# Turning queries and keys of the neighbourhood attention with VectorE blocks and on-chip transfers instead of TensorE transposes

## What is computed

```
q, k, v = split(h @ w_qkv, 3)                 # 256 x 2048 each, 16 heads of 128
q = rms_norm(q per head, q_gain); k = rms_norm(k per head, k_gain)
s[q, i, j] = q . k(row i, column j of the window) * 128**-0.5 + bias   # 4 rows x 16 columns
out = softmax(s) @ v;   x = x + out @ w_o
```

## Time and profile before

| what | value |
|---|---|
| median of three timed runs | 2403.22 us |
| the profiled execution | 2403.74 us |
| its span (first to last instruction) | 2402.0 us |
| TensorE busy | 2390.1 us, 100% by the page's rounding |
| VectorE busy | 1528.0 us, 64% |
| ScalarE busy | 1225.9 us, 51% |
| GpSimd busy | 106.2 us |
| hardware queue of SyncE's transfers | 58.6% of the 16 DMA engines' span |
| granted TensorE clock | full speed in all slices but a rounding |

### The profile page before, as it was taken

One profiled execution on the slowest core, in us unless ns is written; L12 is line 12 of the kernel. 1 busy time (PEld: TensorE's weight loads), 2 busy tenths in 40 slices (PEclk: granted clock), 3 DMA queues, 4 the chain that ended last, 5 costly groups with the idle time before them and its releaser, 6 DMA issues.

```text
span 2402.0 us, 30494 instructions
## 1 busy us (share of the span) xinstructions
PE 2390.1 (100%) x12340; PEld 2045.0 (85%) x12340; DVE 1528.0 (64%) x1788; ACT 1225.9 (51%) x1597; POOL 106.2 (4%) x117
## 2 busy tenths in 40 slices
PE   8999999999999999999999999999999999999999
PEld 7998988788888888888877888888888888888887
DVE  6767866577567657667666655655655654564654
ACT  6555455555445445545565655555443443443442
POOL 0221410000000000000000100000000000000000
PEclk9999999999999999999999999999999999999999
DMA  9566786555655656655655665555556566666664
GB/s 307 152 170 175 167 206 206 167 186 191 202 183 181 206 174 196 201 178 189 216 183 167 187 190 171 158 175 185 184 193 193 183 196 193 191 190 195 185 202 149
DMA packets 327068, 451.69 MB, mean 188 GB/s; under 512 B 14464, under 2 KB 209280, under 8 KB 326288
## 3 DMA queue, kind: packets, MB, share of 16 engines
q1 hardware_dynamic: 324640, 440.52, 58.6%
q0 software_dynamic: 2144, 9.22, 2.4%
q10 hardware_dynamic: 144, 0.01, 0.0%
HBM read 446.54 MB, written 2.10 MB: 187 GB/s over the span
## 4 chain that ended last, share of the span: by engine, by line
PE 99%; DVE 0%; DMA 0%; ACT 0%; SPq 0%; issue 0%; POOL 0%; DVEq 0%
PE main L585 94%; PE aux L585 3%; PE aux L598 1%; PE aux L699 0%; PE aux L717 0%; DMA RAW<-in_w_in 0%; DVE LO L1189 0%; DVE AR L1192 0%; DVE XT L1192 0%; PE aux L683 0%; DVE AR L1189 0%; PE aux L659 0%; ACT HI L834 0%; PE aux L608 0%; SPq L529 0%
## 5 line engine op out<-in xcount | busy, mean ns | idle before, releaser
L1189 DVE TENSOR_TENSOR LO<-RAW,HI 128x1024 fp32r<-128x1024 f32 (+2 forms) x833 | 1010.7, 1236 | 594.7 <-ACT HI L834 594.2
L834 ACT ACTIVATE HI<-RAW 128x1024 fp32r<-128x1024 f32 (+2 forms) x833 | 851.2, 1045 | 642.8 <-PE main L585 591.9
L585 PE MATMUL main<-XT,HI 128*128 128x512 f32 x2944 | 739.5, 393 | 0.0
L585 PE MATMUL main<-HI,YT 128*128 128x512 f32 x2240 | 693.2, 389 | 0.0
L585 PEld LDWEIGHTS main<-XT,HI 128*128 128x128 f32 x2944 | 530.0, 189 | 95.6 <-issue 0.2
L585 PEld LDWEIGHTS main<-HI,YT 128*128 128x128 f32 x2240 | 420.5, 188 | 86.9
L585 PE MATMUL main<-HI,XT 128*128 128x512 f32 (+1 forms) x1472 | 456.2, 385 | 7.6 <-DVE LO L1189 7.6
L585 PE MATMUL main<-LO,YT 128*128 128x512 f32 x1120 | 435.8, 389 | 0.0
L585 PEld LDWEIGHTS main<-XT,LO 128*128 128x128 f32 x2944 | 401.6, 190 | 28.8
L585 PE MATMUL main<-XT,LO 128*128 128x256 f32 x2944 | 410.4, 282 | 0.0
L585 PEld LDWEIGHTS main<-HI,XT 128*128 128x128 f32 x1472 | 274.8, 188 | 58.4 <-DVE XT L1192 7.0
(11 more groups left out here) (91 smaller groups left out, 730.1 us busy)
## 6 DMA issues: line engine op xcount, KB each, us to landing
RAW<-in_mlp_w SPq DMA_DIRECT2D x256, 512.0 KB, 4.2
RAW<-in_w_up SPq DMA_DIRECT2D x176, 512.0 KB, 4.9
RAW<-in_na_w_qkv SPq DMA_DIRECT2D x96, 512.0 KB, 4.4
RAW<-in_w_in SPq DMA_DIRECT2D x95, 512.0 KB, 4.6
RAW<-in_w_down SPq DMA_DIRECT2D x88, 512.0 KB, 4.6
RAW<-in_w_out SPq DMA_DIRECT2D x32, 512.0 KB, 4.5
RAW<-in_w_ple_gate SPq DMA_DIRECT2D x32, 512.0 KB, 4.5
RAW<-in_na_w_o SPq DMA_DIRECT2D x32, 512.0 KB, 4.2
```

The source lines that it names most:

```text
L585: return L.e.matmul(out, l, r, start=start, stop=stop, skip_group_check=True)
L834: return L.e.activation(out, x, f, **kw)
L1189: return L.e.tensor_tensor(out, x, y, op)
```

## The change

Queries and keys no longer go through TensorE to be turned.

- VectorE multiplies into one QN and then does one transpose instruction on it that turns each 32 by 32 block in place within the block's 32 partitions, into QB (128 partitions, 4 pieces of a head, 256). For the queries the order within a block is reversed.
- SyncE carries the blocks to their partitions: 16 transfers from SBUF to SBUF for each query or key block, each of 32 partitions with two runs of 512 bytes, into QL (queries; the place of SQN) or KG (keys). They stand in SyncE's queue ahead of the fetch of the ninth slot after the block's last (`turned_heads`), behind a wait for VectorE's transpose. For the four groups these are fetches 464, 488, 512, 536 (queries) and 472, 496, 520, 544 (keys).
- The two gains and 128**-0.5 are multiplied into one vector, once (`head_gains`), and put on the queries alone: ScalarE copies QL to QG with that scale at slot j0 + 13 (`n_gain`, 128x1024).
- `n_score` reads the keys of a head in five runs of 32, 128 elements apart, and waits for ScalarE's `n_gain` and for the transfers of the keys. Scores and norms move one slot later, the first two heads' probabilities from j0 + 24 to j0 + 26 and their products from 26 to 27, the other two's from 26 and 28 to 27 and 29.
- TensorE's and VectorE's `n_turn` are gone, all 16 of each. ScalarE's squares of a key block wait for `n_gain` of the group, VectorE's transpose waits until the transfers before it have landed.

```diff
         for grp in range(4):
             j0 = 448 + 24 * grp
-        for i in range(2):
-            for t in range(2):
-                put(mid, j0 + 10 + 8 * i + t + (grp + i == 0), "n_turn", grp, i, t)
+        put(mid, j0 + 13, "n_gain", grp)
...
+            def turned_heads(grp, i):
+                L.wait_ge(S("v_nt"), 2 * grp + i + 1)
+                if grp and i:
+                    L.wait_ge(S("p_ns"), 4 * grp)
+                for p in range(4):
+                    for d in range(4):
+                        dst = (QL, KG)[i][32 * d:32 * d + 32].rearrange("p (t c) n -> p t c n", t=2)[:, :, p if i else 3 - p, :]
+                        src = QB[32 * p:32 * p + 32, d, :].rearrange("p (t n) -> p t n", t=2)
+                        L.e.dma_start(dst, src).then_inc(S("d_nt"), 16)
+
+            moved = {b.last + 9: b.what[1:] for b in blocks if b.what[0] == "qk"}
             for j in range(len(slot)):
                 if j < 4:
                     turned_input(j)
+                if j in moved:
+                    turned_heads(*moved[j])
                 fetch(j)
...
-                q, k = QG[grp % 2][:, hh, :], KG[grp % 2][:, hh, :]
+                q, k = QG[:, hh, :], KG[:, :, 32 * hh:32 * hh + 32]
                 out = take("n_score", h)
-                L.wait_ge(S("v_nx"), 4 * grp + 4)
-                mm(out[:, 0:160], q[:, 0:128], k[:, 96:256], True, True)
-                mm(out[:, 160:320], q[:, 128:256], k[:, 0:160], True, True).then_inc(S("p_ns"), 1)
+                L.wait_ge(S("a_ng"), grp + 1)
+                L.wait_ge(S("d_nt"), 512 * grp + 512)
+                mm(out[:, 0:160], q[:, 128:256], k[:, 3:8, :], True, True)
+                mm(out[:, 160:320], q[:, 0:128], k[:, 0:5, :], True, True).then_inc(S("p_ns"), 1)
...
+            def n_gain(grp):
+                L.wait_ge(S("v_gk"), 1)
+                L.wait_ge(S("d_nt"), 512 * grp + 256)
+                if grp:
+                    L.wait_ge(S("p_ns"), 4 * grp)
+                act(QG.rearrange("p h (g n) -> p g h n", n=32), QL.rearrange("p g (h n) -> p g h n", n=32), ACT.Copy, scale=gqk).then_inc(S("a_ng"), 1)
...
-                    if i > 1:
-                        L.wait_ge(S("p_nt"), 2 * (i - 2) + 2)
-                    tt(QN[i % 2], p8, bc(nr, 2, 128), ALU.mult).then_inc(S("v_nn"), 1)
+                    if i:
+                        L.wait_ge(S("v_nt"), i)
+                    tt(QN, p8, bc(nr, 2, 128), ALU.mult).then_inc(S("v_nn"), 1)
+                    L.wait_ge(S("v_nn"), i + 1)
+                    if i:
+                        L.wait_ge(S("d_nt"), 256 * i)
+                    turned = QB.rearrange("p k (m n) -> p k m n", n=32)
+                    L.e.transpose(turned if i % 2 else turned[:, :, :, ::-1], QN.rearrange("p m (k n) -> p k m n", n=32)).then_inc(S("v_nt"), 1)
```

More of the change, by code:

```diff
@@ L216, in stages @@
         j0 = 448 + 24 * grp
-        for i in range(2):
-            for t in range(2):
-                put(mid, j0 + 10 + 8 * i + t + (grp + i == 0), "n_turn", grp, i, t)
+        put(mid, j0 + 13, "n_gain", grp)
         for h in range(4 * grp, 4 * grp + 4):
-            put(mid, j0 + 21, "n_score", h)
+            put(mid, j0 + 22, "n_score", h)
         for h in range(4 * grp, 4 * grp + 4):
-            put(mid, j0 + 22, "n_norm", h)
+            put(mid, j0 + 23, "n_norm", h)
         for h in range(4 * grp, 4 * grp + 2):
-            put(mid, j0 + 24, "n_prob", h)
+            put(mid, j0 + 26, "n_prob", h)
         for h in range(4 * grp, 4 * grp + 2):
-            put(mid, j0 + 26, "n_out", h)
+            put(mid, j0 + 27, "n_out", h)
         for h in range(4 * grp + 2, 4 * grp + 4):
-            put(mid, j0 + 26, "n_prob", h)
+            put(mid, j0 + 27, "n_prob", h)
         for h in range(4 * grp + 2, 4 * grp + 4):
-            put(mid, j0 + 28, "n_out", h)
+            put(mid, j0 + 29, "n_out", h)
     for kp, j in ((0, 568), (1, 568), (2, 569), (3, 569), (4, 570), (5, 570), (6, 576), (7, 576)):
@@ L284, in stage @@
             take(("f_out", rest[0]), ("v_fyl", rest[0] + 1))
-        elif name == "n_turn":
-            take(("n_turn",) + rest, ("v_nx", 4 * rest[0] + 2 * rest[1] + rest[2] + 1))
         elif name == "n_score":
@@ L402, in program @@
         VN = ar(4096, 2, D)
-        QN = [ar(8192 + i * 1024, 8, 128) for i in range(2)]
-        QG = [ar(10240 + i * 1024, 4, T) for i in range(2)]
-        KG = [ar(12288 + i * 1024, 4, T) for i in range(2)]
+        QN, QB = ar(8192, 8, 128), ar(9216, 4, 256)
+        QG, KG = ar(10240, 4, T), ar(11264, 8, 128)
         BIS = ar(14336, NBI, 512)
@@ L409, in program @@
         PTN = [ar(16896 + i * 512, 320) for i in range(2)]
-        SQN = ar(17920, 8, 128)
-        nss, nl, nr = small(128, 8), small(136, 8), small(144, 8)
+        SQN, QL = ar(17920, 8, 128), ar(17920, 8, 128)
+        nss, nl, nr, gqk = small(128, 8), small(136, 8), small(144, 8), small(212, 1)
         HD = [ar(4096 + i * 512, 2, T) for i in range(4)]
@@ L753, in tensor_engine @@
             work = {"e": gate_value, "turn": turn, "xq": turn_half, "h_score": h_score, "h_far": h_far, "h_out": h_out, "h_turn": h_turn, "f_sums": f_sums, "f_score": f_score,
-                    "f_turn": f_turn, "f_out": f_out, "n_turn": n_turn, "n_score": n_score, "n_prob": n_prob, "n_out": n_out,
+                    "f_turn": f_turn, "f_out": f_out, "n_score": n_score, "n_prob": n_prob, "n_out": n_out,
                     "spread": spread}
@@ L1032, in scalar_engine @@
                     "gate": gate, "gate_sq": gate_sq,
-                    "root2": root2, "rb": rb, "e_out": e_out, "n_score": n_score, "n_prob": n_prob, "n_out": n_out}
+                    "root2": root2, "rb": rb, "e_out": e_out, "n_gain": n_gain, "n_score": n_score, "n_prob": n_prob, "n_out": n_out}
             def beside(what):
@@ L1144, in evacuate @@
                         L.wait_ge(S("v_nr"), i)
+                    if i % 2:
+                        L.wait_ge(S("a_ng"), k[1] + 1)
                     for t in range(2):
@@ L1424, in f_out, with head_gains @@
                    ALU.subtract).then_inc(S("v_fyl"), 1)
[L1426 to L1438, removed]
+            def head_gains():
+                L.wait_ge(S("d_col"), 16)
+                L.e.tensor_scalar(gqk, COL[:, P_QG:P_QG + 1], COL[:, P_KG:P_KG + 1], SCALE, ALU.mult, ALU.mult).then_inc(S("v_gk"), 1)
             def n_score(h):
@@ L1464, in vector_engine @@
                     "xl": turn_half, "gate_sum": gate, "gate_root": gate_root, "gate_res": gate_res, "gate_gain": gate_gain, "n_root": n_root,
-                    "last_half": last_half, "resid": resid, "gained": last_gained, "root2": root2, "n_turn": n_turn, "n_score": n_score, "n_norm": n_norm, "n_out": n_out}
+                    "last_half": last_half, "resid": resid, "gained": last_gained, "root2": root2, "bias0": head_gains, "n_score": n_score, "n_norm": n_norm, "n_out": n_out}
             def beside(what):
```

## The result

The changed kernel takes 2433.03 us (2431.94 to 2434.13), the kernel before 2403.20 (2402.84 to 2403.93): ratio 1.0124, interval 1.0113 to 1.0136. It is 29.8 us slower, where the prediction said 5.8 us faster, and lies outside its range.

The account below looks back on a forecast made before the run. TensorE was taken as the bound, busy 2390.1 of 2402.0 us. Transposes -7.4 plus stall 1.5 made -5.9 us: 2397.8 against the profiled execution, 2397.3 by the median, stated as 2397.4; range 2395.3 to 2404.5 us.

Parts of the forecast that it names:

- the 7.4 us of the transposes: TensorE's stream: removing 64 transposes, 16 groups at 0.46 us each, saves 7.4 us.
- the block transpose: VectorE, right behind QN: eight instructions of 1024 columns, 1.2 us each (bounds 0.6 and 2.5), hidden in idle time.
- ScalarE's gain copy: ScalarE: four copies of 1024 columns, about 1.05 us each, hidden in that engine's idle time.
- the scores' runs of 32: TensorE's scores: reading the moving side in runs of 32 elements costs zero, bound 0.1 us in all.
- the stall at slot 464: Queries of group 0: TensorE waits 1.5 us for VectorE's LO of slot 464 behind the transfers.
- the fourth rival: Transfers run one after another: 33.6 us a block, stalls 194 us, time 2590 us; chance 0.02.
- I take 0.50: SyncE's queue: each of 16 transfers takes 0.50 us to issue, 8.0 us a block, with ends 6.6 and 11.2.
- third rival: SyncE's queue becomes the bound: at 0.70 us an issue, stalls 14.8 us, time 2410.6 us; chance 0.12.
- The fetches behind the late one catch up: SyncE's queue after the transfers: fetches issue 0.41 us apart while each slot lasts 2.72 us.
- Later scores, probabilities and products cost the same where they now stand: Attention steps moved to later slots: no added cost, zero; the tightest has one slot (2.72 us) for its writing.
- The "No stall" for the scores: Scores after slot 494: last key transfer issued at 1438.8, landing 2.1 to 3.3 us later, so TensorE doesn't wait.
- The rule that was weighed: SyncE's issues: a fixed 512 cycles a copy would mean 0.41 us each, a 6.6 us hold and 0.1 us stall.

## Why the prediction was wrong

**Right:** the 7.4 us of the transposes (7.5 by the run with one transfer); the block transpose (1.2 forecast, 1.25); ScalarE's gain copy and the scores' runs of 32 at nothing; the place and kind of the stall at slot 464; the overlap of the transfers, which excludes the fourth rival.

**The step that failed first: "I take 0.50, as the transfers' patterns are like the first pair: 16 x 0.50 = 8.0 us".** It is 0.64 us and 10.2 to 11.0. The working itself carries this far: with 0.64 us slot 464 waits 1.5 + 2.2 = 3.7 us and each other query slot 10.2 - 8.0 - 0.5 = 1.7, in all 8.8; the landing, counted from the issue, is 4.1 us and not the 3.7 taken for all fetches, which adds 0.4 to each, 10.4 in all. 12.0 were measured at these four slots. That makes 2403.2 - 7.4 + 10.4 = 2406.2, with the prediction's own third rival (0.70 us) at 2410.6. So the issue time, by the prediction's way of counting, explains under a third of the 37.1 us that the transfers cost. (The 3.7 us was row 10's, of slot 488; the fetch of slot 464 itself had taken 5.0 us to land in the kernel before. It takes 4.1 in the changed one, so this reading cost the sum little.)

**The step that failed with it: "The fetches behind the late one catch up: they are issued 0.41 us apart, and each slot lasts 2.72 us".** They do so for TensorE, which waits once for late weights. But the first of them is issued 10 us later than before, and on ScalarE and VectorE it pushes everything that is listed behind its split. "Later scores, probabilities and products cost the same where they now stand" was checked against the engines' times and not against their order behind a late split. The run with twelve transfers isolates this: its queue is held 7.6 to 8.6 us, as predicted, and it takes 17.2 us more than expected. The "No stall" for the scores failed by the same road: the transfers landed in 1.9 us, faster than the 2.1 to 3.3 taken, but they were issued 0.64 us apart and, behind the late squares of the key block, began late. TensorE waited for them four times, 4.4 us in all. That wait, and the distance of 0.64 us, are two of the signs that the prediction had named as making it wrong.

**What was not in the sum: the clock.** A wait was priced at its length. The prediction had no term for what follows it: in the five stretches shown above TensorE is busy for 4.6 + 4 x 3.4 = 18.2 us at half the clock, so some 9.1 us are lost to it (an estimate, half of that busy time). Three of the stretches lie at query slots (slots 464, 488 and 536), one behind the probabilities of group 0 (a wait of 3.0 us, until 1391.41) and one at the scores of group 2 (2.0 us, until 1537.57). In the run with the keys alone a wait of the same 3.0 us was followed by no such stretch, so the length of a wait alone doesn't tell.

The changed kernel against the run with one transfer, start of slot to start of slot from 456 to 551, is 37.1 us longer (the waits, and what follows each of them):

| where | us |
|---|---|
| first query slot of a group behind the late fetch | 12.6 |
| the two slots behind it, at the lower clock | 5.8 |
| scores, and the slot behind them | 8.1 |
| slots j0 + 26 and j0 + 27, probabilities and the weights behind them | 9.8 |
| the rest | 0.7 |

The lines add up to the 37.1 but for rounding, and 37.1 - 7.4 is the 29.7 of the result. Only the first line was forecast, at 1.5. Seen the other way, the 37.1 are 23.7 us of waits, some 9.1 of the lower clock, and 4.3 that are neither.

**The rule that was weighed** was the Trainium skill's 512 cycles for each copy instruction (DMA: Bandwidth & Descriptors, section "Why a DMA increments its semaphore by 16 and not by 1"). The trace does not show one fixed cost: a lone fetch takes 368 ns, one in a row 468, a transfer inside SBUF 597. The sum had set it aside; what was wrong was to take the pairs as the nearest row with a spread of only 0.45 to 0.53, where no row showed a transfer from SBUF to SBUF.

**Still open:** why the clock fell behind some waits and not behind others of like length; whether a full reordering of both engines' lists would save all 16 transfers on SyncE (only one step was moved). The price of the lower clock is read from rows and was not run by itself, and the 4.3 us that are neither wait nor clock were not followed.

## What to carry to other kernels

Before an operation goes ahead of a prefetch in an in-order queue, price it by a row of its own kind, and if there is none, let the range and the likeliest case reach to its dearest neighbour. Then follow not one late fetch to the one slot that reads it but every instruction listed behind that slot on each engine: here the late slots of each group delayed its scores and probabilities, which had nothing to do with weights. If such a burst can't be made smaller, split it over two queues: eight and eight gave 2396.56 us where sixteen in one gave 2433.03.

## What the runs showed of the hardware

- A transfer from SBUF to SBUF, one in a row of them, holds SyncE's queue for 0.63 to 0.68 us, with 16 to 128 KB, one run or two, 32 or 128 partitions. The fetch right behind a row of them takes 586 ns, the next ones 467 or 468, a lone one 368.
- GpSimd issues such transfers at 539 ns each. 16 in a row land in 5.7 us in the median; eight beside eight of SyncE's in 2.2, both queues taken together.
- TensorE's granted clock fell to the 1.2 GHz level at 1350.9, inside a wait that lasted from 1348.55 to 1353.13, and was back at 1357.8; until then the products started 0.43 us apart in place of 0.227. Four more such stretches of 3.4 us stand behind waits of 2.0 to 3.0 us. With the keys' transfers alone the longest wait of this part is 3.0 us as well, and the clock stayed at 1.00.
